# One change in four parts to a two-block transformer kernel: chunk loads placed between value panels, state products of two directions apart, head norms over 8 columns, modulation panels in another order

## What is computed

```
mod = silu(c) @ w_mod + b_mod                    # 24 panels of 256 columns: shifts, scales, gates
p   = modulate(rmsnorm(x), ...) @ w_in           # gates of two directions, values, q, og, u, v, ga, gb
o_f, o_b = chunked linear attention, forward and backward, 4 heads, 4 chunks of 64 tokens
o_a = rmsnorm(o_f + o_b, g_norm_a) * silu(og)    # the head norm: mean of squares over a head's channels
...                                              # spatial gating, swiglu feed-forward
mod_2[l] = silu(c_2) @ mod_w_2[l] + mod_b_2[l]   # 24 panels for each of 2 layers; kv_mod: 8 panels
layer 0: gated linear attention (one direction, 4 heads of 256 values, head norm), then PEER
layer 1: sliding-window attention (swa_q, softmax, swa_out), then PEER
PEER: queries -> 8 x 16 of 16384 experts; gelu(h @ u_tab) weighted by the routes @ v_tab
```

## Time and profile before

| what | value |
|---|---|
| median of 3 runs | 2567.52 us (2563.28 to 2568.8) |
| the profiled execution | 2567.99 us, span 2566.2 us |
| mean granted TensorE clock | 0.983 of full |
| PE / PEld / DVE / ACT / POOL busy | 97% / 87% / 70% / 48% / 3% |
| PE's two longest groups, L670 and L745 | 771.7 and 703.8 us |
| loaded | 468.5 MB, 183 GB/s over the span |

### The profile page before, as it was taken

The page is one execution under the profiler, slowest core; times in us unless marked ns, Lnnn a source line. Parts: engine busy times, 40 slices in busy tenths (PEclk is TensorE's granted clock), DMA queues, the critical chain, the costliest instruction groups (busy, mean ns, idle before and its releaser), DMA issues.

```text
span 2566.2 us, 42626 instructions
## 1 busy us (share of the span) xinstructions
PE 2481.5 (97%) x15700; PEld 2225.2 (87%) x15700; DVE 1791.7 (70%) x3484; ACT 1238.7 (48%) x2429; POOL 79.2 (3%) x42
## 2 busy tenths in 40 slices
PE   7999999999999999999999998899999999999997
PEld 4587889988899999998888887789999999788886
DVE  5562559867369967785888874749977787755554
ACT  2322134442235567774454553434557776455454
POOL 0000000000140000000000000041000000000000
PEclk9999999999999999999999999999999999999998
DMA  6462457747234553435788863133554344655552
GB/s 266 164 248 84 178 194 274 250 175 272 101 114 169 180 175 137 147 134 194 279 288 286 288 235 142 61 132 133 182 181 146 136 145 148 236 191 195 196 192 103
DMA packets 79173, 471.65 MB, mean 184 GB/s; under 512 B 8832, under 2 KB 9088, under 8 KB 26160
## 3 DMA queue, kind: packets, MB, share of 16 engines
q1 hardware_dynamic: 78480, 467.85, 51.5%
q10 hardware_dynamic: 272, 1.05, 0.1%
q0 software_dynamic: 272, 0.69, 0.1%
HBM read 468.51 MB, written 1.05 MB: 183 GB/s over the span
## 4 chain that ended last, share of the span: by engine, by line
PE 90%; DVE 6%; DMA 2%; ACT 1%; issue 1%; SPq 0%; DVEq 0%; ACTq 0%
PE bank L670 27%; PE bank L745 27%; PE bank L532 6%; PE bank L881 5%; PE bank L682 4%; PE bank L795 4%; PE bank L697 3%; PE bank L912 2%; PE bank L542 2%; PE bank L516 1%; PE bank L974 1%; PE bank L1017 1%; DMA ring<-in_peer_v 1%; PE bank L793 1%; PE bank L548 1%
## 5 line engine op out<-in xcount | busy, mean ns | idle before, releaser
L670 PE MATMUL bank<-h_split,t_split 128*128 128x256 f32 x6144 | 771.7, 285 | 4.7 <-DVE t_split L1907 4.5
L670 PEld LDWEIGHTS bank<-h_split,t_split 128*128 128x128 f32 x6144 | 745.4, 192 | 6.6 <-DVE t_split L1907 5.9
L1907 DVE TENSOR_TENSOR t_split<-ring,t_split 128x1024 fp32r<-128x1024 f32 x512 | 624.4, 1221 | 159.0 <-ACT t_split L1190 155.2
L745 PE MATMUL bank<-t_split,w_split 128*128 128x512 f32 x3072 | 703.8, 391 | 6.3 <-ACT w_split L1197 6.3
L745 PEld LDWEIGHTS bank<-t_split,w_split 128*128 128x128 f32 x3072 | 580.1, 189 | 128.6 <-ACT w_split L1197 7.1
L1195 ACT ACTIVATE t_split<-ring 128x1024 fp32r<-128x1024 f32 x256 | 271.8, 1062 | 359.1 <-PE bank L745 222.4
L1190 ACT ACTIVATE t_split<-ring 128x1024 fp32r<-128x1024 f32 x256 | 271.1, 1059 | 294.0 <-PE bank L670 270.6
L1939 DVE TENSOR_TENSOR w_split<-arena,w_split 128x256 fp32r<-128x256 f32 x256 | 108.7, 424 | 205.6 <-ACT w_split L1197 205.2
L1117 ACT ACTIVATE arena<-bank 128x256 f32<-128x256 f32 (+2 forms) x160 | 64.0, 404 | 318.0 <-PE bank L697 69.2
L881 PE MATMUL bank<-h_split,wd_split 128*128 128x256 f32 x1056 | 128.2, 284 | 4.0 <-ACT h_split L1417 4.0
L881 PEld LDWEIGHTS bank<-h_split,wd_split 128*128 128x128 f32 x1056 | 127.3, 191 | 5.1 <-issue 4.3
(11 more groups left out here) (308 smaller groups left out, 2746.9 us busy)
## 6 DMA issues: line engine op xcount, KB each, us to landing
ring<-in_peer_u SPq DMA_DIRECT2D x128, 1024.0 KB, 4.9
ring<-in_peer_v SPq DMA_DIRECT2D x128, 1024.0 KB, 4.9
ring<-in_w_mod SPq DMA_DIRECT2D x24, 1024.0 KB, 6.0
ring<-in_mod_w SPq DMA_DIRECT2D x24, 1024.0 KB, 4.9
H<-in_mod_w SPq DMA_DIRECT2D x96, 256.0 KB, 5.1
ring<-in_w_in SPq DMA_DIRECT2D x22, 1024.0 KB, 5.1
ring<-in_w_up SPq DMA_DIRECT2D x22, 1024.0 KB, 4.9
ring<-in_peer_wq SPq DMA_DIRECT2D x16, 1024.0 KB, 4.9
```

What stands on the lines that cost most here:

```text
L670: last = mm(bank[:, 0:T], u[:, a_, k, :], h_split[:, b_, k, :], start=(k == 0 and a_ + b_ == 0), stop=(k == KT - 1 and a_ == 1))
L745: last = mm(BK[2 * tt + hf][:, :], w_split[:, j, a_, tt * P:(tt + 1) * P], t_split[:, 1 - j, b_, hf * 512:(hf + 1) * 512], start=(first an ...
L1907: TT(t_split[:, 1 - j, 1, :].rearrange("p (k c) -> p k c", k=KT), ring[:, r, :].rearrange(view, k=KT, j=2)[:, j], t_split[:, 1 - j, 0, :]. ...
```

## The change

1. V stage: SP places each chunk of modulation panels directly behind the value panel of the same two blocks. Before, the first pair's four chunks (eight loads, 2 MB) stood ahead of the third value panel. The stage of layer 0 now sums four panels of `mod_w0`, then `kv_mod`, then 16 of `mod_w1`.
2. `lin_states` can do one direction; in the two-direction attention a projection tile, or `lin_out(0)` for head 1, stands between the directions.
3. The head norms sum squares into 8 columns (token block by head), with the squares as weights and one column of ones. DVE and ACT take 1/sqrt of these 8 columns, DVE multiplies them into 8 identity matrices, and PE spreads them with 8 matmuls (`lin_spread`).
4. Modulation panels: a fourth pair behind the fourth `w_in` panel, none behind the last ones of the context part; one pair inside the heads in three pieces; two pairs (before: eight single panels) in GLA's projections; two pairs between the `swa_out` panels, in halves behind the residual tiles, with a `mod_fold(4)` of their own.

```diff
-                    + [(a["w_in"], 1, "proj", 2), (a["w_mod"], 2, "mod_acc", 1)] * 3
-                    + [(a["w_in"], 1, "proj", 2)]
+                    + [(a["w_in"], 1, "proj", 2), (a["w_mod"], 2, "mod_acc", 1)] * 4
                     + [(a["w_in"], 1, "proj", 4), (a["w_mod"], 2, "mod_acc", 1)] * 2
-                    + [(a["w_in"], 2, "proj", 2), (a["w_mod"], 2, "mod_acc", 1)] * 2
-                    + [(a["w_in"], 10, "proj", 2)]
+                    + [(a["w_in"], 8, "proj", 2), (a["w_mod"], 2, "mod_acc", 1), (a["w_in"], 6, "proj", 2)]
...
-                    + [(a["gla_qk"], 1, "proj", 2), (a["mod_w0"], 1, "mod_acc", 1)] * 4
-                    + [(a["gla_v"], 1, "proj", 2), (a["mod_w0"], 1, "mod_acc", 1)] * 4
+                    + [(a["gla_qk"], 2, "proj", 2), (a["mod_w0"], 2, "mod_acc", 1), (a["gla_qk"], 2, "proj", 2)]
+                    + [(a["gla_v"], 2, "proj", 2), (a["mod_w0"], 2, "mod_acc", 1), (a["gla_v"], 2, "proj", 2)]
...
-                       (a["swa_q"], 4, "proj", 2), (a["swa_out"], 4, "proj", 2)]
+                       (a["swa_q"], 4, "proj", 2)]
+                    + [(a["swa_out"], 1, "proj", 2), (a["mod_w1"], 2, "mod_acc", 1)] * 2 + [(a["swa_out"], 2, "proj", 2)]
...
-                src, n0 = (a["kv_mod"], 0) if layer == 0 else (a["mod_w1"], 20)
+                src, n0 = (a["mod_w0"], 20) if layer == 0 else (a["mod_w1"], 20)
                 for c in range(4):
+                    v_panel(c // 2, c % 2)
                     v_mod(src, n0, c)
-                for r in range(2):
-                    v_panel(0, r)
...
-            def lin_states(m, h, dirs, E, vcols, behind):
+            def lin_states(m, h, dirs, E, vcols, behind, only=None):
-                for d in range(dirs):
+                for d in range(dirs) if only is None else (only,):
...
-                for pair in range(2):
-                    for hh in range(2):
-                        h = 2 * pair + hh
+                for h in range(HEADS):
+                    for tt in range(2):
                         for x in range(E):
-                            last = mm(BK[pair][:, hh * T:(hh + 1) * T], ones, osq[:, h * E + x, :],
+                            last = mm(BK[0][:, 2 * h + tt:2 * h + tt + 1], osq[:, h * E + x, tt * P:(tt + 1) * P], ones[:, 0:1],
...
+            def lin_spread(diag):
+                pe.wait_ge(sems["odiag"], e.more("odiag"))
+                for n in range(8):
+                    last = mm(BK[n // 4][:, n % 4 * P:(n % 4 + 1) * P], ones, diag[:, n * P:(n + 1) * P], start=True, stop=True)
+                last.then_inc(sems["orep"], 1)
...
-            lin_states(M1, 0, 2, 1, v1, 1)
+            lin_states(M1, 0, 2, 1, v1, 1, 0)
+            x_tiles(1)
+            lin_states(M1, 0, 2, 1, v1, 2, 1)
             for h in range(HEADS):
                 if h + 1 < HEADS:
                     lin_turns(M1, h + 1, 2)
                     lin_scores(M1, h + 1, 2)
                     x_tiles(1)
-                    lin_states(M1, h + 1, 2, 1, v1, 1)
-                x_tiles(1)
+                    lin_states(M1, h + 1, 2, 1, v1, 1, 0)
+                if h:
+                    x_tiles(1)
+                if 0 < h < HEADS - 1:
+                    lin_states(M1, h + 1, 2, 1, v1, 2, 1)
                 lin_out(M1, h, 2, 1, v1, lambda d, h: S0[:, d, h, :])
+                if h == 0:
+                    lin_states(M1, 1, 2, 1, v1, 1, 1)
             x_tiles(1)
             lin_squares(M1, 1)
-            x_tiles(7)
+            x_tiles(2)
+            lin_spread(M1["tB"])
+            x_tiles(5)
...
-                for pair in range(2):
-                    ins = TS(root_buf[:, pair * 512:(pair + 1) * 512], BK[pair][:, :], 1.0 / dv, EPS, MUL, ADD)
-                ins.then_inc(sems["ovar"], 1)
+                TS(stats, BK[0][:, 0:8], 1.0 / dv, EPS, MUL, ADD).then_inc(sems["ovar"], 1)
                 dve.wait_ge(sems["ostd"], e.more("ostd"))
-                dve.reciprocal(root_buf, root_buf).then_inc(sems["dve_step"], 1)
+                dve.reciprocal(stats, stats).then_inc(sems["dve_step"], 1)
                 dve.wait_ge(sems["dve_step"], e.stepped())
+                TT(diag.rearrange("p (n q) -> p n q", n=8), ident.unsqueeze(1).broadcast_to([P, 8, P]),
+                   stats.unsqueeze(2).broadcast_to([P, 8, P]), MUL).then_inc(sems["odiag"], 1)
...
             gates(1)
+            mod_between(2, 0)
             scans(1)
...
+            def mods_behind(k):
+                if k % 2 == 0:
+                    used(1)
+                mod_between(2, 16, k % 2 * 4, k % 2 * 4 + 4)
+            residual("proj", 16, {k: lambda k=k: mods_behind(k) for k in range(4)})
+            used(2)
+            mod_out((modc[:, 32:40], 0, V("mod_b_2")[:, 80:88]))
```

More of the change, by code:

```diff
@@ L183, in build @@
                   "q_hi", "q_lo", "hi", "split", "lb", "gate", "gates_f", "logf", "expo", "exps", "lin_in",
-                  "scores", "masked", "dstate", "state", "o_sum", "o_bank0", "o_bank1", "osq", "oms", "ovar", "ostd",
+                  "scores", "masked", "dstate", "state", "o_sum", "o_bank0", "o_bank1", "osq", "oms", "ovar", "ostd", "odiag", "orep",
                   "o_done", "wctx", "s0", "s0_in", "vln", "sgu", "merged", "rows", "y_out", "out_done", "trig",
@@ L1088, in _ @@
             oS = kt(M4["oS"], 8)
-            proj_cols(4, lambda k: oS[:, k, :], T)
+            for n in range(4):
+                proj_cols(1, lambda k: oS[:, k, :], T)
+                if n < 2:
+                    mod_between(2)
+                if n == 2:
+                    mod_fold(4)
             peer(1)
@@ L1647, in mod_first, with mod_between @@
                 mod_uses[0] += 1
-            def mod_between(n, c_col):
-                slots = []
-                for _ in range(n):
-                    r = panel[0] % RING
-                    panel[0] += 1
-                    dve.wait_ge(sems[f"loaded{r}"], e.more(f"loaded{r}", 16))
-                    slots.append(r)
+            slots = []
+            def mod_between(n, c_col, first=0, last=KT):
+                if first == 0:
+                    slots.clear()
+                    for _ in range(n):
+                        r = panel[0] % RING
+                        panel[0] += 1
+                        dve.wait_ge(sems[f"loaded{r}"], e.more(f"loaded{r}", 16))
+                        slots.append(r)
                 wrapped = n == 2 and slots[1] < slots[0]
@@ L1660, in mod_between @@
                 acc, turned = macc[:, 0:n, :], (nrm[:, 0:2, :] if n == 2 else macc[:, 1:2, :])
-                TS(acc, w[:, :, 0, :], cact[:, c_col:c_col + 1], None, MUL).then_inc(sems["dve_step"], 1)
-                dve.wait_ge(sems["dve_step"], e.stepped())
-                for k in range(1, KT):
-                    ins = STT(acc, w[:, :, k, :], cact[:, c_col + k:c_col + k + 1], acc, MUL, ADD)
+                for k in range(first, last):
+                    col = cact[:, c_col + k:c_col + k + 1]
+                    ins = TS(acc, w[:, :, 0, :], col, None, MUL) if k == 0 else STT(acc, w[:, :, k, :], col, acc, MUL, ADD)
                     if k < KT - 1:
@@ L1667, in mod_between @@
                         dve.wait_ge(sems["dve_step"], e.stepped())
+                if last < KT:
+                    return
                 ins.then_inc(sems["mod_acc"], n)
@@ L1793, in gated @@
                     gate_block(b)
-                roots(root_buf, dv)
+                roots(M3["dec"][:, 16:24], root_buf, dv)
+                dve.wait_ge(sems["orep"], e.more("orep"))
                 for b in range(8):
@@ L2185, in _ @@
             e.tiles("proj", 4)
-            used(10)
+            used(6)
             for _ in range(2):
@@ L2303, in _ @@
             dve.wait_ge(sems["dve_step"], e.stepped())
-            for n in range(4):
-                used(1)
-                mod_between(1, 16)
+            used(2)
+            mod_between(2, 16)
+            used(2)
             e.tiles("proj", 8)
@@ L2312, in _ @@
             TT(M3["kd0"], M3["kd0"], M3["k"], MUL).then_inc(sems["lin_in"], 1)
-            for n in range(4):
-                used(1)
-                mod_between(1, 16)
-            mod_out((modc[:, 32:48], 0, V("mod_b_2")[:, 32:48]))
+            used(2)
+            mod_between(2, 16)
+            used(2)
+            mod_out((modc[:, 32:40], 0, V("mod_b_2")[:, 32:40]))
             used(4)
```

93 lines of the change are left out of this document (51 added, 42 removed).

## The result

| | before | after |
|---|---|---|
| median of 12 runs of each, us | 2565.82 | 2569.68 |
| lowest to highest, us | 2560.09 to 2571.15 | 2562.47 to 2573.75 |
| ratio, with 95% interval | | 1.0017 [1.0010, 1.0024] |
| the profiled execution: time, span, us | 2567.99, 2566.2 | 2570.25, 2568.5 |

The change costs about 4.4 us (2565.8 x 0.0017). I had forecast -3.5 us, "no change, on the fast side". By the bound of 0.2% it is no change, but on the slow side, and its interval leaves out both zero and my -3.5.

The account below looks back on a forecast made before the run. PE, busy for 97% of the span, was taken to bound the kernel. Terms -13.0 - 5.2 - 2.9 + 4.3 + 6.0 + 7.3 = -3.5 us against 2567.5 gave 2564.0 us, range 2557.5 to 2573.5.

Parts of the forecast that it names:

- no change, on the fast side: Whole kernel: -3.5 us to 2564.0 us, inside the 0.2% (5.1 us) a measurement can tell; forecast's chance 0.48.
- V stages: Both layers' V stages: PE's waits at the third value panel and the lower clock behind go, 2 x 6.5 = -13.0 us.
- state products: Two-direction attention: a tile fills PE's four waits of 1.3 us for DVE's read of direction 0, -5.2 us.
- head norms: Mixer and GLA: PE's squares cost 0.3 and 0.5 us more, spreading 3.6; +4.3 us (bounds +2 and +5).
- `w_in` phase: Last context panel: new PE wait of 4.3 us, x tiles start near 148.2 instead of 142.16; +6.0 us.
- GLA -2.9: GLA's projections: PE's wait for `gla_qk` panel 3, issued behind a modulation panel waiting for DVE, goes; -2.9 us.
- `swa_out` +7.3: `swa_out`'s third panel: new PE wait of 4.4 us, 2.0 for the clock, 0.9 for the added fold.
- my rival on them: Head norms: one-column matmuls nearly free, so the squares' 6.0 us vanish, 2558.0 us; chance 0.04.
- The rival that the third value panel still comes late: V stages: PE still waits at the third value panel and all 13.0 us stay, 2577 us; chance 0.09.
- the rival of panels that land early: `w_in` and `swa_out`: panels behind a modulation panel land 4.9 us after issue; 5.8 us less, 2558.2 us; chance 0.20.

Follow-up runs that it names:

- with 64 columns: The whole change, with each head-norm sum of squares by a matmul of 64 equal columns instead of one: 1.0001 [0.9991, 1.0010].
- V alone: Kernel before with only the V stages' order changed, each modulation chunk issued right behind the value panel of the same blocks: 0.9954, -11.8 us.
- that half: Kernel before with only the last `w_in`-phase pair summed in three pieces behind heads 0 to 2, five pairs staying among the context panels: 1.0002.
- V and S together: Kernel before with the V stages' new load order and the two directions' state products apart: 0.9931, 2548.72 us against 2565.26.
- the context pair alone: Kernel before with only the fourth modulation pair among the context panels, one pair less among the x tiles: 1.0027, +6.9 us.
- G alone: Kernel before with only GLA's modulation panels in two pairs, four panels moved to V stage 0, and `mod_w1` 16 to 19 between `swa_out` panels: 1.0013, +3.3 us.

## Why the prediction was wrong, step by step

| part | I had, us | measured alone, us (95%) |
|---|---|---|
| V stages | -13.0 | -11.8 (-15.1 to -8.2) |
| state products | -5.2 | -6.7 (-9.2 to -4.1) |
| head norms | +4.3 | +8.7 (+5.4 to +12.1) |
| `w_in` phase | +6.0 | +8.5 (+5.1 to +11.5) |
| GLA -2.9 and `swa_out` +7.3 | +4.4 | +3.3 (+1.0 to +5.6) |
| sum | -3.5 | +2.0 |

The parts' sum of +2.0 agrees with the +4.4 of the whole within such intervals. One term lies outside its interval, and it carries 4.4 of the 5.5 us between the two sums. From my -3.5 to the +4.4 of the whole it is 7.9 us, so that term does not carry all of it: with 64 columns the whole stands at 1.0001 (-2.3 to +2.6 us), still above -3.5.

**Head norms: the term that failed.** I wrote "Sum 0.3 + 0.5 + 3.6 = +4.3 (bounds +2 and +5)". The work itself I priced a little high: the squares take 1.71 us (247.69 to 249.40) and 3.49, not 2.0 and 4.0, and the spreading 1.78 twice as said. That makes 3.6 us. What failed is that the sum ended there: I counted PE's time in these matmuls and put what they do to its clock at nothing. The term was +4.3, and alone it measured +8.7. Bound and rivals missed it as well; my rival on them only asked whether they might be cheaper. With 64 columns the part falls from +8.7 to +1.8 us, and the whole change from 1.0017 to 1.0001. The traces show 1.7 us of that as a slower clock in the whole change and 3.4 in the part alone; the rest stands only in the times. The Trainium skill (TensorE: Matmul & The Clock Gate, "Wait — 56ns, not 53.3ns?"), whose floor of 25 ns I weighed, is not reached: a one-column record takes 3.49 / 32 = 109 ns here, a 64-column one 3.51 / 32 = 110, a 128-column one 1.78 / 16 = 111. So the row, and not this floor, gave nearly the right price for that work.

**V stages: right.** Waits gone, 6.2 us in each stage of the kernel with V alone, granted clock 1.00 from 1204 to 1216 us. In the whole change the first stage gains only 5.0: a wait of 0.8 us for ACT at 1281 stands there (in V and S together one of 1.2, with V alone none). The rival that the third value panel still comes late is out.

**State products: right.** No wait is left before them. DVE's pieces behind the heads hide: with these pieces and the old order PE waits the same four times 1.3 us, and that half costs nothing measurable (1.0002).

**`w_in`: mechanism and size right, details not.** The step had one wait of 4.3 us at the last context panel; there are two, 1.8 and 2.1, because the panel before is held up as well. The last one is issued at 122.30 and used at 129.32, 7.0 us later, as I took it. The x tiles start at 145.65, not 148.2, partly since DVE's gates came at 114.00 instead of 116.42: the fall of the clock at 98 us, which the earlier trace rows carry as 15.68 us, did not occur in this execution. So the +3.5 between the two starts is not the price. Seven of the eleven traces with the old order of the context panels have no such fall, V and S together for one:

```profile
97.33 14.00 PE L531 MATMUL bank<-H,ring 128*128 128x512 f32 x32 [2.31 <-DMA ring<-in_w_in]
...
139.70 3.69 PE L794 MATMUL bank<-H,ring 128*128 128x256 f32 x16 [0.35 <-ACT arena L1123]
```

From the first of these rows to the second it is 42.4 us, and 48.3 in the whole change (97.37 to 145.65): +5.9. Against the four old-order traces that have the fall (44.1) it is +4.2. By the times the part costs +8.5 and the context pair alone +6.9 (+4.4 to +9.5). My +6.0 is in both intervals, and the rival of panels that land early is out: behind a modulation panel they took 7.0 us.

**GLA: right, and lost again.** G alone gains the 2.9 us. In the whole change they are given back by the clock at GLA's start, behind the late modulation panel of the FFN. PE's row before the FFN starts 0.5 us later than before (348.87 for 348.35), its row of GLA's value panels 4.0 later (602.51 for 598.48), although the 2.9 us are gone in between: the episode took some 6 us. No term of mine had it, and in the trace of the whole change it is the largest piece that I did not have, larger than the 1.7 us behind the squares. What it weighs in the medians is not known: the norms alone with 64 columns have it in their trace as well and measured +1.8 in all. That panel is late in the traces of four of the six kernels that hold the new norms, and in none of the ten that don't. Nothing of the norms runs at that time, but the traces show one thing beside it. In all six a packet of the profile's instruction queue (q8, 0.02 MB) stands within 0.05 us of that panel's issue, and SP's next issue takes 0.95 to 1.44 us, which is the packet's own time within 0.03 us. In all ten others the packet comes 5.0 to 6.0 us behind the issue, and SP's next issue takes 0.43. The four with the late panel have the four longest of these packets (1.27 to 1.43 us). This fits a load of instructions that the added code moved to this place; no experiment moved it, so the cause is not shown.

**`swa_out`: right.** I had a wait of 4.4 us and 7.3 in all; it waits 4.2 and takes 7.7.

So the sign came out wrong because I let three gains and three losses of similar size decide it by their difference, and one loss, the head norms, was half of what it measured: +8.7 for +4.3 turns -3.5 into +0.9. The other 3.5 us up to the +4.4 lie within the intervals of the single parts, so what they are stays open; the late panel of the FFN is the candidate that the trace shows.

## What to carry to other kernels

A part that removes waits of the bounding engine (here an order of loads, and one tile put between two dependent products) is worth its waits, and the clock behind them where it fell; test it by itself, since the same edit's other parts can eat all of it. An engine that is not waited for (DVE here, 18 us less work) pays nothing back, and each matmul added on PE for its sake is paid in full. When a matmul is made narrow to save work, look at how long the wide one takes first: here a record takes 109 to 111 ns from 1 to 128 columns, and the one-column ones cost clock.

## What the hardware did that I had not expected

- PE was busy all the time, with 32 one-column matmuls in 3.5 us, and the granted clock fell from 2.4 to 1.2 GHz behind them; with 64 columns, at the same pace, it stayed at 2.4 GHz. Until then I had looked for falls of the clock only behind waits. The Trainium skill (TensorE: Matmul & The Clock Gate, "What's actually happening") says that the gate is set by how busy PE has been; a busy share of 4.00 us in 4.00 did not keep the clock up here, so what the profile calls busy is not all that it goes by.
- A load of 1 MB took 6.9 us instead of 4.8 to be used, and SP's next issue 1.44 us instead of 0.43, at a place where the change had altered nothing; the trace has a packet of the instruction queue at that very issue, and in the kernel before 5.5 us behind it. That this packet is the cause is not shown.
